# Block 2's gated scans: where their decays, states and squares stand in the order of the work

## The reference, cut to what matters

```python
def _gla_scan(q, k, v, log_a, s0):
    # chunked: S_t = diag(alpha_t) S_(t-1) + k_t^T v_t, o_t = q_t S_t
    ...
def _gla_bidirectional(ctx_in, lat_in):
    ...
    la = log_sigmoid(r @ w_d + b_d) / 16          # decays, both directions, rank 16
    o_cf, s_f = _gla_scan(qc, kc, vc, lfc, s0)    # context, from zero
    o_cb, s_b = _gla_scan(flip(qc), flip(kc), flip(vc), flip(lbc), s0)
    o_lf, _ = _gla_scan(ql, kl, vl, lfl, s_f)     # x, from the context's states
    o_lb, _ = _gla_scan(flip(ql), flip(kl), flip(vl), flip(lbl), s_b)
```

## Time and profile before

| | us |
|---|---|
| median of three runs | 2108.84 |
| the profiled execution | 2111.18 |
| its span | 2109.4 |
| TensorE busy, matmuls | 2067.0 |
| VectorE busy | 1356.6 |
| ScalarE busy | 956.0 |
| GpSimd busy | 135.3 |
| granted TensorE clock, mean | 0.993 |

### The profile page before, as it was taken

How to read it: one execution, slowest core, us unless ns; L and a number is a source line. 1 busy time by engine, 2 the same in 40 slices (tenths; PEclk the granted TensorE clock), 3 DMA queues, 4 the chain that set the end, 5 groups by cost and what they waited for, 6 DMA issues and landing times.

```text
span 2109.4 us, 31385 instructions
## 1 busy us (share of the span) xinstructions
PE 2067.0 (98%) x12082; PEld 1783.0 (85%) x12082; DVE 1356.6 (64%) x2381; ACT 956.0 (45%) x1568; POOL 135.3 (6%) x140
## 2 busy tenths in 40 slices
PE   9999999999999999999999999999999989999998
PEld 6779988778999888888888778888878889888997
DVE  6756667767876328568435555868565588575665
ACT  4545555555555434353323463223244454445443
POOL 1001000000110100000200001111110000100100
PEclk9999999999999999999999999999999999999999
DMA  8436656424555422212222104534234334251553
GB/s 248 146 126 250 226 214 203 168 98 164 187 180 182 131 99 70 71 62 79 71 99 84 67 21 152 181 129 143 97 130 150 106 119 146 90 180 54 194 172 131
DMA packets 79731, 285.79 MB, mean 135 GB/s; under 512 B 8976, under 2 KB 9628, under 8 KB 79584
## 3 DMA queue, kind: packets, MB, share of 16 engines
q1 hardware_dynamic: 71136, 256.93, 36.0%
q10 hardware_dynamic: 6416, 19.51, 2.5%
q0 software_dynamic: 2032, 7.35, 1.3%
HBM read 277.92 MB, written 5.83 MB: 135 GB/s over the span
## 4 chain that ended last, share of the span: by engine, by line
PE 82%; DVE 9%; ACT 5%; issue 2%; POOL 0%; DMA 0%; DVEq 0%; ACTq 0%; SPq 0%
PE pb L1065 16%; PE pb L1067 16%; PE pb L1066 16%; PE pb L1078 6%; PE pb L1079 6%; PE pb L1080 6%; DVE SPL L2117 3%; PE pb L1084 2%; PE pb L1244 2%; PE pb L1321 2%; PE pb L1245 2%; PE pb L1246 2%; ACT SPH L1551 2%; PE pb L1424 2%; PE pb L1405 2%
## 5 line engine op out<-in xcount | busy, mean ns | idle before, releaser
L2117 DVE TENSOR_TENSOR SPL<-RAW,SPH 128x1024 fp32r<-128x1024 f32 x460 | 560.0, 1232 | 392.5 <-ACT SPH L1551 370.9
L1065 PE MATMUL pb<-HTH,SPH 128*128 128x256 f32 (+1 forms) x2008 | 648.1, 323 | 12.5 <-DVE SPL L2117 6.1
L1067 PE MATMUL pb<-HTH,SPL 128*128 128x256 f32 (+1 forms) x2008 | 639.3, 318 | 0.0
L1066 PE MATMUL pb<-HTL,SPH 128*128 128x256 f32 (+1 forms) x2008 | 639.3, 318 | 0.0
L1551 ACT ACTIVATE SPH<-RAW 128x1024 fp32r<-128x1024 f32 x462 | 478.2, 1051 | 238.8 <-PE pb L1067 119.5
L1065 PEld LDWEIGHTS pb<-HTH,SPH 128*128 128x128 f32 x2008 | 384.5, 191 | 41.9 <-issue 8.5
L1066 PEld LDWEIGHTS pb<-HTL,SPH 128*128 128x128 f32 x2008 | 384.8, 192 | 26.4
L1067 PEld LDWEIGHTS pb<-HTH,SPL 128*128 128x128 f32 x2008 | 384.4, 191 | 26.0
L1078 PE MATMUL pb<-SPH,HTH 128*128 128x512 f32 x640 | 255.1, 399 | 0.5 <-DVE QNB L2558 0.5
L1079 PE MATMUL pb<-SPH,HTL 128*128 128x512 f32 x640 | 250.6, 392 | 0.0
L1080 PE MATMUL pb<-SPL,HTH 128*128 128x512 f32 x640 | 250.6, 392 | 0.0
(11 more groups left out here) (284 smaller groups left out, 2486.9 us busy)
## 6 DMA issues: line engine op xcount, KB each, us to landing
RAW<-in_w_up SPq DMA_DIRECT2D x88, 512.0 KB, 4.5
RAW<-in_wa SPq DMA_DIRECT2D x64, 512.0 KB, 3.3
RAW<-in_w_in SPq DMA_DIRECT2D x48, 512.0 KB, 4.9
RAW<-in_wmg SPq DMA_DIRECT2D x48, 512.0 KB, 3.3
RAW<-in_wbr SPq DMA_DIRECT2D x48, 512.0 KB, 3.2
RAW<-in_w_down SPq DMA_DIRECT2D x44, 512.0 KB, 4.5
RAW<-in_w_ada SPq DMA_DIRECT2D x24, 512.0 KB, 4.6
ARAW<-in_w_ada ACTq DMA_DIRECT2D x24, 512.0 KB, 4.3
```

Source lines behind the costliest of these rows:

```text
L1065: T.matmul(o, wh[:, kt, :], xh[:, kt, n0:n1], start=kt == 0, stop=False)
L1066: T.matmul(o, wh[:, kt, :], xl[:, kt, n0:n1], start=False, stop=False)
L1067: m = T.matmul(o, wl[:, kt, :], xh[:, kt, n0:n1], start=False, stop=kt == 7)
L2117: W.tensor_tensor(lo, raw, hi.bitcast(F32), SUB).then_inc(*dve.tick(s["lo_dve"], ("u", u)))
```

## The change

The scan is cut into generators of its own. The decays go in four steps instead of three: the minima move from `gdec2` to `gln`, the last exp to a new step `gexp`. E4 gets other addresses: it now lies over GW's kinds 0 and 3, not 2 and 3, so that the turned keys (over kinds 1 and 2) may still be in use. In layer 1 the scan begins between the key weights; both scans' decays now stand before branch a. In layer 0 the first scan's decays and `ginit` stand in the second value group. The states come in five steps behind all turned keys, and in layer 1 behind the second scan's decays. The first scan's squares and root (`rows_norm`) stand in doublings 2 to 4 of the second. The decay weights of layer 1 are loaded at the end of layer 0. The rings and the spacing (`IC`, `PC`, `KEYS`, `GAPS`) change with it. No instruction on data is added or taken away but that `gsq` is cut in two steps.

```diff
--- before.py
+++ after.py
@@ -33,8 +33,9 @@
 LO4, HI4, LOW6, LOW7, ALL8 = (0, 1, 2, 3), (4, 5, 6, 7), (0, 1, 2, 3, 4, 5), (0, 1, 2, 3, 4, 5, 6), (0, 1, 2, 3, 4, 5, 6, 7)
 
 RA = [2.0, 1.25]
-IC, PC = (4, 5), (8, 17)
-KEYS = ((0,) * 8, (2, 1, 1, 2, 2, 2, 2, 1))
+IC, PC = (4, 6), (3, 1)
+GAPS = ((1, 2), (2, 3))
+KEYS = ((0, 0, 0, 0, 1, 1, 1, 2), (1, 3, 3, 3, 2, 1, 1, 1))
 LOWEST = -30.0
 EARLY = 3
 FIRST = 11
@@ -555,66 +556,97 @@
             self.give(n)
             yield
 
+    def decays(self, l, s, ring):
+        self.add("mark", f"gla{l}{s}")
+        for i in range(4):
+            self.take(ring, ("gd", l, s, i))
+            self.add("gdec", l, s, i)
+        yield
+        self.add("gdec2", l, s)
+        yield GAPS[l][0]
+        self.add("gln", l, s)
+        for i in range(4):
+            self.give(("gd", l, s, i))
+        yield GAPS[l][1]
+        self.add("gexp", l, s)
+        yield
+
+    def doubling(self, l, s, ring, late=iter(())):
+        full = gla_full(s, l)
+        if full:
+            for hp in range(2):
+                self.take(ring, ("gp", l, s, -1, hp))
+            self.add("gprod", l, s, -1)
+            yield LEAD[l][s]
+        for j in range(SPANS + full):
+            if full and j < SPANS:
+                for hp in range(2):
+                    self.take(ring, ("gp", l, s, j, hp))
+            if full:
+                self.add("keep", l, s, j - 1)
+                for hp in range(2):
+                    self.give(("gp", l, s, j - 1, hp))
+            if j < SPANS:
+                if full:
+                    self.add("gprod", l, s, j)
+                self.add("gwiden", l, s, j)
+            if 2 <= j < 5:
+                next(late, None)
+            yield IC[l] if full else 1
+
+    def keys_turned(self, l, ring):
+        for i in range(4):
+            n = self.take(ring, ("ke", l, i))
+            self.add("gke", l, i)
+            self.give(n)
+            if i % 2:
+                yield
+
+    def states(self, l, ring):
+        for i in range(5):
+            if i < 4:
+                self.take(ring, ("st", l, i))
+                self.add("gst", l, i)
+            if i:
+                self.add("gst2", l, i - 1)
+                self.give(("st", l, i - 1))
+            yield
+
+    def outputs(self, l, s, ring):
+        for h in range(5):
+            if h < 4:
+                self.take(ring, ("go", l, s, h))
+                self.add("gout", l, s, h)
+            if h >= 1:
+                self.add("gout2", l, s, h - 1)
+                self.give(("go", l, s, h - 1))
+            yield
+
+    def rows_norm(self, l, s):
+        for t in range(2):
+            self.add("gsq", l, s, t)
+            yield
+        self.add("gnorm", l, s)
+        yield
+
     def gla(self, l, ring):
-        for s in (1, 0):
...
+        yield from self.decays(l, 1, ring if l else LO4)
+        self.add("ginit", l, 1)
+        yield
+        yield from self.doubling(l, 1, ring)
+        yield from self.keys_turned(l, ring)
+        if gla_full(1, l):
+            yield from self.states(l, ring)
+            yield from self.outputs(l, 1, ring)
+        yield from self.decays(l, 0, ring)
+        if not gla_full(1, l):
+            yield from self.states(l, ring)
+        yield PC[l]
+        self.add("ginit", l, 0)
+        yield
+        yield from self.doubling(l, 0, ring, self.rows_norm(l, 1) if gla_full(1, l) else iter(()))
+        yield from self.outputs(l, 0, ring)
+        yield from self.rows_norm(l, 0)
 
     def branch_a(self, l, ring):
         for ft in range(8):
@@ -785,9 +817,9 @@
         H = ("x1", "c1") if last else ("x0", "c0")
         if not last:
             self.add("mark", "x1done")
-        self.add("wdec", l)
         early = []
         if not last:
+            self.add("wdec", l)
             self.limit = self.gets + EARLY - 1
             for ft in range(EARLY):
                 self.take((0, 1, 2, 3), ("gk", l, ft))
@@ -809,18 +841,20 @@
         self.add("rank", l, u, H)
         self.put_w(u)
         self.give(n)
+        scan, steps = self.gla(l, HI4), iter(KEYS[l])
         for ft in range(len(early), 4):
             u = self.get_w(f"wgk{l}", ft)
-            n = self.take(ALL8, ("gk", l, ft))
+            n = self.take(LO4 if last else ALL8, ("gk", l, ft))
             self.add("gk_mm", l, ft, u, None)
             self.put_w(u)
             self.add("gk", l, ft)
             self.give(n)
+            if last:
+                next(scan)
         if not last:
             drain(self.gla_queries(0, H))
-        scan, steps = self.gla(l, HI4), iter(KEYS[l])
         for g in range(2):
-            for _ in self.group_n(("gv", l, g), f"wgv{l}", g, (0, 1, 2, 3), LO4 if last else ALL8, H):
+            for _ in self.group_n(("gv", l, g), f"wgv{l}", g, (0, 1, 2, 3), HI4 if g and not last else LO4, H):
                 for _ in range(next(steps)):
                     next(scan)
             for t in range(4):
@@ -906,6 +940,7 @@
         self.give(n)
         self.split_upto(self.gets + 1)
         self.add("stats", "c1")
+        self.add("wdec", 1)
 
     def x_out(self, l, t):
         self.add("x_out", l, t)
@@ -1762,17 +1797,19 @@
 
     def gdec2(l, st):
         for d in range(2):
-            e = sb["E4"][:, 2 * d:2 * d + 2, :].rearrange("p a n -> p (a n)")
+            e = sb["E4"][:, 3 * d, :]
             act.wait_ge(s["gla_dve"], ("z", l, st, d))
             A.activation(e, e, ACT.Exp, scale=-1.0).then_inc(*act.tick(s["gla_act"], ("ex", l, st, d)))
 
     def gln(l, st):
         for d in range(2):
-            e = sb["E4"][:, 2 * d:2 * d + 2, :].rearrange("p a n -> p (a n)")
+            e = sb["E4"][:, 3 * d, :]
             act.wait_ge(s["gla_act"], ("ex", l, st, d))
             act.wait_ge(s["const_dve"], "one")
             A.activation(e, e, ACT.Ln, scale=1.0, bias=sb["ONE"][:, 0:1]).then_inc(
                 *act.tick(s["gla_act"], ("ln", l, st, d)))
+
+    def gexp(l, st):
         for d in range(2):
             et = sb["ET"][:, d, :]
             act.wait_ge(s["gla_dve"], ("la", l, st, d))
@@ -1782,6 +1819,8 @@
         k.past(act, f"gla{l}{st}", SCAN)
         spilled(act, k, l)
         act.wait_ge(s["gla_dve"], ("la", l, st, 1))
+        if st == 0:
+            act.wait_ge(mm, ("st", l, 3))
         for ft in range(4):
             act.wait_ge(*k.read(("gk", l, ft)))
         for kind in (KF, KB):
@@ -1832,15 +1871,16 @@
...
-    def gsq(l, st):
+    def gsq(l, st, t):
         k.past(act, f"gla{l}{st}")
...
+        if st == 0 and gla_full(1, l):
+            act.wait_ge(s["gla_dve"], ("gr", l, 1))
+        for h in range(4):
...
@@ -2391,25 +2431,29 @@
     def gdec2(l, st):
         k.past(dve, f"gla{l}{st}", SCAN)
         spilled(dve, k, l)
-        for op, o in ((MAX, sb["E4"]), (MIN, sb["ET"][:, :, :].rearrange("p d (i n) -> p (d i) n", i=2))):
-            for i in range(4):
-                name = ("gd", l, st, i)
-                dve.wait_ge(mm, name)
-                for hh in range(2):
-                    c = slice(hh * 256, hh * 256 + 256)
-                    end = (dve.free(*k.read(name)) if op == MIN and hh else
-                           dve.tick(s["gla_dve"], *([("z", l, st, i // 2)] if op == MAX and hh and i % 2 else [])))
-                    W.tensor_scalar(o[:, i, c], k.P(name)[:, c], par("b_dec", l * 8 + i * 2 + hh), LOWEST, ADD,
-                                    op).then_inc(*end)
+        for i in range(4):
+            dve.wait_ge(mm, ("gd", l, st, i))
+            for hh in range(2):
+                c = slice(hh * 256, hh * 256 + 256)
+                W.tensor_scalar(sb["E4"][:, i // 2 * 3, i % 2 * 512 + hh * 256:i % 2 * 512 + hh * 256 + 256], k.P(("gd", l, st, i))[:, c], par("b_dec", l * 8 + i * 2 + hh),
+                                LOWEST, ADD, MAX).then_inc(
+                    *dve.tick(s["gla_dve"], *([("z", l, st, i // 2)] if hh and i % 2 else [])))
 
     def gln(l, st):
+        for i in range(4):
+            name = ("gd", l, st, i)
+            for hh in range(2):
+                c = slice(hh * 256, hh * 256 + 256)
+                W.tensor_scalar(sb["ET"][:, i // 2, i % 2 * 512 + hh * 256:i % 2 * 512 + hh * 256 + 256],
+                                k.P(name)[:, c], par("b_dec", l * 8 + i * 2 + hh), LOWEST, ADD, MIN).then_inc(
+                    *(dve.free(*k.read(name)) if hh else dve.tick(s["gla_dve"])))
         for d in range(2):
             et = sb["ET"][:, d, :]
             dve.wait_ge(s["gla_act"], ("ln", l, st, d))
             for i in (2 * d, 2 * d + 1):
                 dve.wait_ge(*k.read(("gd", l, st, i)))
             W.scalar_tensor_tensor(out=et, in0=et, scalar=-LOWEST,
-                                   in1=sb["E4"][:, 2 * d:2 * d + 2, :].rearrange("p a n -> p (a n)"), op0=ADD,
+                                   in1=sb["E4"][:, 3 * d, :], op0=ADD,
                                    op1=SUB).then_inc(*dve.tick(s["gla_dve"], ("la", l, st, d)))
 
```

(48 more changed lines are left out.)

1 line of the change is left out of this document (removed).

## The result

Eleven runs of the changed kernel have a median of 2115.41 us (2112.11 to 2117.62), eleven of the kernel before, taken beside them, 2109.41 (2105.60 to 2111.35). The ratio is 1.0029, 95% interval 1.0021 to 1.0037: 6.0 us slower, where 7.3 us faster was forecast. The time lies 7.9 us above the range.

A forecast was written before the change was run, and what follows sets the result against it. TensorE, busy 98% of the span, was taken as the bound, so only its waits and lower clock could be won. Minus 3.75, minus 9.9, plus 4.8, plus 1.6 gave minus 7.3 us: 2101.5 from the median, range 2093.5 to 2107.5.

The forecast's parts named there:

- The five stages: Layer 0's values and branch a, layer 1's rank and gk products, values and branch a; forecast sum minus 7.25 us.
- rival C: Layer 1's group boundary: `gexp` falls behind one more split, 7.2 us more than forecast, 2108.7 us; chance 0.07.
- Part 1: Layer 0, first scan's decays under the values' second group: the wait before its doublings goes, minus 2.95 us.
- Part 2: Layer 0, second scan: minus 1.40 us from earlier `ginit`, squares hidden, root plus 0.6 us.
- Part 3: Layer 1, decay weights loaded ahead: directly 0 us, and `gdec` can run behind the first GK product.
- Part 4: Layer 1, second scan's decays under the values' second group: branch a's waits and lower clock go, minus 9.9 us.
- Part 5: Layer 1, first scan packed into the values' first group: new boundary wait plus 4.8 us, lower clock plus 1.6.

The follow-up runs named there:

- e3_squares: Changed kernel with layer 0's first-scan squares, root and normalisation put back behind that scan's outputs: 2115.85 us, ratio to before 1.0039.
- e6_later: e3_squares with layer 0's second scan started two half weights later after its decays: 2112.26 us, ratio to before 1.0017.
- e9_ginit: e5_turns and e6_later together, but with the pause of two half weights behind `ginit` instead of ahead of it: 2100.21 us, ratio 0.9962.
- e5_turns: Changed kernel with the spill off the decay weights' mark and layer 1's four key turns behind the second group's first weight: 2104.67 us, ratio 0.9980.
- e12_pool: Changed kernel with GpSimd's normalisation alone over 16 of 256 columns, a pricing run that leaves out work: ratio to before 1.0024.

## Why the prediction was wrong

The five stages were to be 7.25 us shorter and are 6.8 longer, 14.0 apart. Nearly every sign that the prediction names for being right came: no waits at the split and ahead of layer 0's doublings, two new ones at the boundary, the lower clock behind them. They watch only what it had thought of. It wasn't rival C either, its one way to be slower: that asks for over 8 us of waiting at the boundary. By its own parts:

- **Part 1, right.** No wait at the first product of layer 0's first doubling.
- **Part 2, failed:** "so they hide". The argument was ScalarE's low load (20.6 of 66 us busy). But the squares stand in its queue ahead of a weight's split, VectorE's low half waits for that split, and the doubling's instructions wait behind the low half; and VectorE was the engine with little reserve, as the same group's 53 of 66 us and the two waits of 1.0 us said. Squares cost 1.64 us, where 0 stood. GpSimd's normalisation, which the root releases, cost 1.94 and was in no term: the step counted the moved instructions of two engines and forgot the third. That leaves 2.6 us. 0.7 of them are the second scan's `gdec`, which takes 1.68 us instead of 0.95, because its last bank waits for the copy of the outputs; every kernel with the new order has that wait. For the other 1.9 the cause stays open. I read them as VectorE's backlog: the doubling starts some 20 us earlier in branch a than before, and e3_squares, e6_later and e9_ginit have the wait at different places. The root, for which 0.6 was taken and 2 allowed, was never taken out by itself and may be in it. Together layer 0 came to plus 2.4 us instead of minus 3.75, an error of 6.2.
- **Part 3, failed:** its price was put at 0, and `gdec` was to run behind the first of the four GK products, at 1604.7. The standstill began at 1604 and lasted 4.6 us, and the clock cost 1.4. The rows had the clue: ScalarE's copy waited 6.26 us for the load, but nothing said that another DMA, issued just ahead of it, would take over as the mark. The step asked when the load lands, not what its reader waits for. Plus 6.0 us, where 0 stood.
- **Part 4, right.** Branch a of layer 1 fell by 12.4 us, of which 2.8 is `gdec` and turns moved out: 9.6 against 9.9. Line 1356's waits there are 0.2 us.
- **Part 5, right in place and wait, short in the clock.** 3.65 and 1.58 us start to start, 5.2 against 4.8, and 0.34 in a slower product behind; `gke`'s wait is on VectorE's doubling and the second on ScalarE's value copy, as said. The stage rose 9.7, of which 1.8 are the four turns (one `gdec` left the stage and one came); so the boundary cost 7.9 against 6.4. The difference is 6.8 us at the lower clock instead of one short stretch: 2.4 us, within the bounds given (0 to 3.4), beyond the 1.6 taken.

6.2, 6.0, 1.5 and 0.3 make the 14.0. The Trainium skill's rule on idle gaps (TensorE: Matmul & The Clock Gate, Why this matters for your kernels) says that a long idle gap between bursts of products sets the array back to half rate. The rows agree: the granted clock is 0.50 from 1652.5 us on, behind 3.5 us of standstill and before the first turn starts at 1652.66. What fell is the prediction's way of reading it, by which the turns would save the clock: they, and the 1.3 us of standstill behind them, lie within the slow stretch already. e5_turns has 2.1 us idle before branch a and no lower clock behind it. And the next activation still follows a table load at once (1663.85 + 1.28, then 1665.15): no drain between them is seen.

Not settled: what the last 1.9 us of layer 0 are, and whether they could be hidden; no kernel took the root out alone or tried fewer instructions per doubling. That the change's gains need all its parts wasn't tried either; they are read from waits that vanished.

## What to carry to other kernels

When a DMA's issue is moved, look at everything that waits for "the last thing this engine did": the wait may pass to another transfer, and a load that lands 20 us early is still used late. Before placing work "beside" a stage, count it on the engine that has no reserve there, through the queue positions it delays, and count the third engine that it wakes. When a wait disappears but the stage keeps its length (247.5 us in three orders), the wait may be the symptom of a backlog; taking away work, not moving it, is then the test. And when every forecast sign comes and the time doesn't, subtract stage by stage: the loss lies where nobody looked.

## What the runs showed of the hardware

Two-operand products on VectorE and GpSimd, all in SBUF, didn't run beside each other here. In the changed kernel VectorE's two of 512 columns took 2.38 and 0.68 us, and GpSimd's pair 2.84 and 2.87:

```profile
L2494 DVE TENSOR_TENSOR GW<-GW,ET x2: 679/1528/2376, 959.7 to 962.0; 128x512 f32<-128x512 f32 x2
...
L2822 POOL TENSOR_TENSOR GV<-GV,GSS x2: 2841/2856/2870, 955.9 to 958.7; 128x1024 f32<-128x1024 f32 x2
```

With the normalisation at its old place (kernel before) GpSimd's first product, from 916.65 us, took 2.84 us: it fell beside a low half on VectorE (two inputs in SBUF, 916.51 to 917.73). The second took 1.89, beside VectorE's maxima and minima out of PSUM, which took 0.48 each. The Trainium skill (SBUF — State Buffer, SBUF: two separate sides) states an exclusive lock: of a GpSimd instruction and a VectorE one with two inputs in SBUF, the first holds the shared ports to its end and the other stands still. The rows agree: GpSimd's pair ends at 955.90 + 5.67 = 961.57, VectorE's long one at 959.75 + 2.38 = 962.13, so that 0.56 of it lies behind GpSimd's end, about what it takes alone (0.68, in e12_pool). With that rule the prediction could have had a term for GpSimd in layer 0, where 1.94 us were missing.
